# Neighbourhood attention and the filter's small layers run beside two of the three hyena projections, the spectra beside the third; modulation groups are spread over the second block

## The chip, the cores and the metric

One core of a Trainium2 chip runs the whole program in one launch. The metric is device time in microseconds (us) of that core. A core has five engines with queues of their own: TensorE (matmuls; PE, its weight loads PEld), VectorE (DVE), ScalarE (ACT), GpSimd (POOL) and SyncE (SP, which issues nearly all weight loads). Each queue runs in order, and engines wait for one another through semaphores.

## The reference, cut to what matters

Two transformer blocks of two layers each, 256 tokens of width 1024, all float32. Only the even layer (layer 0) of the second block is changed in its computing order; it treats 256 latent and 256 context tokens, 512 columns together:

```python
def na_hyena_mixer(h_lat, h_ctx, ...):                 # layer 0 of the second block
    p = h @ w_in                                       # 1024 x 3072: q, k, v (512 each), x0, x1, v of hyena (512 each)
    a = neighbourhood_attention(qk_norm(q), qk_norm(k), v, k_ctx, v_ctx, rpb)   # 8 heads of 64; context: dense attention
    b = hyena_operator(p[..., 1536:], ...)
    return concatenate([a, b], axis=-1) @ w_out

def hyena_operator(u, conv_w, conv_b, filter_params, d_bias):
    x0, x1, v = split(short_conv(u, conv_w, conv_b), 3)    # taps t-1, t, t+1
    z = v * x1
    filt = hyena_filter(length, *filter_params)            # sin(freq * (h @ fw + fb)) three times, @ fw4, times a window
    y = long_conv(z, filt) + z * d_bias                    # by a Fourier transform: spectra, product, inverse
    return y * x0

# before each layer of the second block, for latent and context alike:
mod = silu(c) @ w_mod[i] + b_mod[i]                    # 1024 x 9216: shift, scale, gate for three places
```

## The kernel before, in words

**Numbers.** Weights and activations of the projections are float32 split into a high and a low float32r part. ACT writes the high part of a weight half block (L1361), DVE the low part (L1651), and TensorE does three matmuls for each 128 x 128 weight tile (L978 to L980): high by high, high by low, low by high. Matmuls of attention, of the filter and of the transforms are plain float32.

**One walk, five engines.** `Engine` holds the order of the work; every engine's class walks it and issues its own instructions, so the order of each queue is the order in which the methods are called. `mark` and `after` turn events into semaphore waits. `fence(who, of)` makes the engines in `who` wait for all that those in `of` have been given so far.

**Projections.** `project_t` (L362) goes through blocks of weights, by default 512 columns by 4 row tiles. Every block has 4 x 4 x 3 = 48 matmuls, and the generator yields after each group of 12. For each finished output tile `evacuate` is called. At the start of a block it calls `paced()` and `prepare`, which loads and splits later blocks. With `wide=256` a block is 256 columns by 8 row tiles: again four yields of 12 matmuls, and an output tile is done at every second yield. Output tiles take PSUM banks from `group` in turn (`Counts.take`); `fresh` waits until the last user of the bank has freed it. There are eight banks of 128 x 512.

**Modulation.** The products with `w_mod` form a generator of 73 steps (`modulations`, L333): 72 times 8 small matmuls on four tiles of `w_mod` (`mod_four`, L1163; 1 MB by four DMAs that SP issues when the last step's matmuls have read the buffers, L2253), every twelfth followed by the closing of a group. `fill(n)` runs n steps; `paced()` runs one at every ninth block (`PACE`); attention pipelines of some stages take them as filler. `modulation(i, j)` (L753) runs steps without pause until group 3i+j is complete, then computes gains, for which ACT waits. Steps 1 to 33 run in the first block of the model.

**The even layer (`even`, L653).** All in one order:
1. q, k, v by `project_t` and `project_n`, banks 0 to 3.
2. The three hyena projections x0, x1, v (two blocks of 48 matmuls each, as q, k and v have; banks 0 to 3). Each output tile goes through `conv`: one ACT instruction with scale and bias (L1540), then two on DVE (L1648) that add the neighbours from the same bank.
3. A fence of all engines, then attention in 16 units (4 pairs of heads by 4 tiles of 128 queries; 512 keys for latent queries, 256 for context ones) through `pipeline` (L307). A unit has six stages, one a round: scores, exp, scale, turn, values, low. In a round the older units go first and a new unit's scores come last. On TensorE a round is: values of unit r-4, turn of unit r-3, scores of unit r. On ACT: copy of values r-4 (L1462), copies of turn r-3 (L1457), the two exponentials of unit r-1 (L1446). On DVE: low part of unit r-5 (L1651, frees the values' bank), reciprocal and diagonals of r-2, bias and maximum of r-1 (L1811, L1813). With `TWO` the scores have two pairs of banks, (3, 4) and (1, 2), the turned halves 5 and 0, the values 6. Every second round has a modulation step (10 in 21 rounds). The scores' weights p have 3 buffers, the turned ones 2. z = v * x1 runs on POOL (L2163) meanwhile.
4. Fences; the loads of the transform matrices, window and filter weights on the ACT queue; z turned (L916); three filter layers, each a matmul (L1214), eight DVE instructions on 64 x 256 (L1941 to L1952) and a sine on ACT (L1549), each followed by a modulation step; the filter's taps (L1224, L1963 to L1967); fence; the spectra of the filter (L1229); fence.
5. `convolution`: spectra of z for both halves s = 0, 1 (L1229), products on DVE (L1989 to L1994) and POOL (L2174, L2176), then the inverse transforms (L1254), each tile followed by three DVE and one ACT instruction (L1648, L2005, L1569, L1651).
6. `modulation(i, 2)` and the output projection "even out", 4 blocks; its rows 0 to 3 are attention's output, 4 to 7 hyena's.

Later, in the odd layer, `modulation(1, 2)` (L753) stands after retention and before the projection "ret out".

**An arrangement like the new one** is in the first block of the model: branch a's attention (`mixing`, L544) with `where=ONE`, scores on one pair of banks (3, 4), runs beside the projections of branch b, 20 groups of 12 matmuls over 13 rounds (256 columns each, half the length of those in the even layer).

Of the kernel before, what the change touches and what calls it, by code (L numbers as in the profile page):

```python
# [109 lines left out]
STRIP, PACE = 266, 9  # L110
# [11 lines left out]
NORM1, NORM2 = 23688, 23552  # L122

# [103 lines left out]
class Engine:  # L227
# [4 lines left out]
    def __init__(self, K, io, mem, banks, sems, e):  # L232
# [8 lines left out]
        self.mod_step, self.fences, self.paces = 0, 0, 0  # L241
# [107 lines left out]
    def paced(self):  # L349

        self.paces += 1
        if self.paces % PACE == 0:
            self.fill(1)
# [299 lines left out]
    def even(self, i, h, N):  # L653
# [7 lines left out]
        OHI, OLO = 4096, 6144  # L661
# [3 lines left out]
        for k, off in enumerate((X0, X1, VV)):  # L665
            run(self.project_t(("hy", k), w, 1536 + 512 * k, 512, h, lambda m, f, k=k, off=off: self.conv(f, A[:, off + m * 512:off + (m + 1) * 512], 4 * k + m)))
        self.fence()
        self.hyena_z()
        rings = self.pair_rings("na", (0, 3072, 24576), 3, 2, 512)
        units = []  # L670
        for r in range(4):
            bi = A[:, 20480 + r * 1024:21504 + r * 1024].rearrange("p (h k) -> p h k", h=2)
            for t in range(4):
                k0, nk = (0, 512) if t < 2 else (256, 256)
                s_ = r * 512 + t * P
                units.append(self.attention(
                    ("na", r, t), A[:, QA + s_:QA + s_ + P], A[:, KA + r * 512 + k0:KA + r * 512 + 512], nk,
                    [A[:, VA + m * 512 + r * P:VA + m * 512 + (r + 1) * P] for m in range(0 if t < 2 else 2, 4)], OHI + s_, OLO + s_, rings,
                    add=bi[:, :, t * 256:(t + 1) * 256] if t < 2 else None, ready="window" if t < 2 else None))
# [12 lines left out]
        cat = self.pair("cat", OHI, OLO, 4, 512)  # L692
        cat2 = self.pair("cat2", 22528, 24576, 4, 512)
        self.convolution(cat2, self.ring("ct", 26624, 2, NT))
        both = self.pair("both", 0, 0, 8, 512)
        both.hi = lambda c, a=0, b=None: (cat.hi(c) if c < 4 else cat2.hi(c - 4))
        both.lo = lambda c, a=0, b=None: (cat.lo(c) if c < 4 else cat2.lo(c - 4))
# [31 lines left out]
    def second_block(self):  # L729
        self.await_context()  # L730
        N = self.norm("second", NORM2, 512)
        for i in range(2):
# [12 lines left out]
            N = self.norm(("b", 0), 8192, 512) if i == 0 else self.norm(("b", 1), NORM2, NT)  # L745
# [147 lines left out]
    load_lambda = load_context = load_window = load_hyena = load_axial = load_decay = await_context = nothing  # L893
    mod_start = mod_four = mod_finish = gains = normed = conv = q_gain = hyena_z = turn_z = filter_layer = filter_end = nothing
    filter_spectra = convolution = axial = silu_out = log_gamma = decay = nothing
# [3 lines left out]
class TensorE(Engine):  # L899
# [296 lines left out]
    def turn_z(self):  # L1196
        for s in range(4):
            f = ("z turn", s)
            out = self.fresh(f, ALL)
            for m in range(4):  # L1200
                mm = self.turn(out[:, m * P:(m + 1) * P], self.A[:, 16384 + m * 512 + s * P:16384 + m * 512 + (s + 1) * P])
            mm.then_inc(*self.mark(("full", f)))

    def filter_layer(self, n):
        e, A, f, FW, HB = self.e, self.A, ("filter", n), 8192, 9664
# [4 lines left out]
        else:  # L1210
            e.wait_ge(*self.after(("filter sin", n - 1)))
            wgt, prev = A[0:64, FW + 256 + 64 * n:FW + 320 + 64 * n], A[0:64, HB + 512 + 256 * ((n - 1) % 2):HB + 768 + 256 * ((n - 1) % 2)]
        out = self.fresh(f, PROJ)[0:64, 0:256]
        e.matmul(out, wgt, prev, start=True, stop=True).then_inc(*self.mark(("full", f)))  # L1214

    def filter_end(self):
        e, A, FW, HB = self.e, self.A, 8192, 9664
        e.wait_ge(*self.after(("filter sin", 2)))
        for m in range(2):
            lt = A[0:64, HB + 512 + m * P:HB + 512 + (m + 1) * P]  # L1220
            for k, way in enumerate(("forward", "backward")):
                f = ("taps", way, m)
                out = self.fresh(f, PROJ)
                e.matmul(out[:, :], lt, A[0:64, FW + 448 + 512 * k:FW + 960 + 512 * k], start=True, stop=True).then_inc(*self.mark(("full", f)))  # L1224

    def forward(self, f, src, kind, n):
        out = self.fresh(f, ALL)
        for m in range(2):
            mm = self.e.matmul(out[:, :], self.A[:, kind * 512 + m * 256 + n * P:kind * 512 + m * 256 + (n + 1) * P], src(m), start=m == 0, stop=m == 1)  # L1229
        mm.then_inc(*self.mark(("full", f)))  # L1230

    def filter_spectra(self):
        A, FIL = self.A, 2048
        self.e.wait_ge(*self.after("dft"))
        for n in range(2):
            for kind in range(2):
                self.forward(("filter spectrum", kind, n), lambda m: A[:, FIL + kind * 1024 + m * 512:FIL + kind * 1024 + (m + 1) * 512], kind, n)

    def convolution(self, cat2, ctb):
        A, ZT = self.A, 18432  # L1240
        for s in range(2):
            for n in range(2):
                for kind in range(2):
# [1137 lines left out]
```

## Time and profile before

| | |
|---|---|
| runs | 3460.04, 3468.54, 3476.8 us; median 3468.54 |
| profiled execution | 3463.9 us, of which the span from first to last instruction is 3462.1 |
| mean granted TensorE clock | 0.949 |
| busy, share of the span | PE 91%, PEld 76%, DVE 48%, ACT 36%, POOL 5% |
| even layer after its norm | from 1752 to 2096 us of the span |
| its hyena projections | about 1821 to 1889 |
| attention | 1889 to 1966 |
| filter to the last inverse transform | 1966 to 2051 |

How to read it: a busy PE is one with matmuls in flight. `PEclk` is the clock that TensorE was granted, 1.00 for 2.4 GHz, 0.50 for 1.2 GHz. In timeline rows the first number is the start in us, the second the length; what stands in brackets is the idle time of the engine before it, and what ended it.

### The profile page before, as it was taken

Reading aid. Unit: us, or ns where it says so; the run is one execution under the profiler, and the core shown is the slowest. Engines: PE = TensorE matmul, PEld = TensorE weight load, DVE = VectorE, ACT = ScalarE, POOL = GpSimd, SP = SyncE. Lnnn points to the kernel's source line nnn. Section 1 sums busy time; section 2 is a strip of 40 time slices with the busy share of each in tenths; the row PEclk is TensorE's granted clock in tenths of the full one; section 3 lists DMA queues with packets and bytes.
Section 4 is the critical chain, followed back from the end, with each engine's and each line's share of the span. In section 5 each row is a group of like instructions: output and inputs, shape, how many; then the busy total and the mean of one; then the engine's idle time right before and its main releaser. Section 6 shows DMA issues by size and latency. Waiting matters only on the chain.

```text
span 3462.1 us, 45581 instructions
## 1 busy us (share of the span) xinstructions
PE 3159.0 (91%) x18558; PEld 2645.2 (76%) x18558; DVE 1673.0 (48%) x2678; ACT 1237.3 (36%) x2073; POOL 161.8 (5%) x181
## 2 busy tenths in 40 slices
PE   6787989987898998999989789999999998996899
PEld 6675979976687997877767457877777777883799
DVE  5554656464565655333374455323443335343465
ACT  4344454433444544222243413212332223233343
POOL 1020000001100000000010010000000000001000
PEclk9898989988999999999999999999999998997999
DMA  4433645642354653232332413233233233241464
GB/s 157 142 104 122 198 166 184 207 159 84 115 187 147 210 197 132 92 110 79 122 125 91 152 47 106 90 109 97 86 122 110 94 108 121 92 158 39 145 204 142
DMA packets 248949, 446.01 MB, mean 129 GB/s; under 512 B 16467, under 2 KB 56804, under 8 KB 247972
## 3 DMA queue, kind: packets, MB, share of 16 engines
q1 hardware_dynamic: 244656, 430.80, 38.4%
q10 hardware_dynamic: 4084, 12.29, 1.0%
q8 instruction: 147, 2.41, 0.3%
q14 instruction: 62, 0.51, 0.0%
HBM read 441.98 MB, written 1.05 MB: 128 GB/s over the span
## 4 chain that ended last, share of the span: by engine, by line
PE 81%; DVE 9%; ACT 4%; issue 2%; DMA 2%; POOL 1%; ACTq 0%; DVEq 0%; POOLq 0%
PE ps L978 22%; PE ps L980 21%; PE ps L979 21%; PE ps L1171 3%; PE ps L1009 2%; PE ps L1010 2%; PE ps L1011 2%; DVE split L1651 2%; DVE AR L1651 1%; PE ps L1119 1%; ACT A L1446 1%; DVE A L1648 1%; DVE A L1701 1%; ACT split L1361 1%; PE ps L1286 1%
## 5 line engine op out<-in xcount | busy, mean ns | idle before, releaser
L978 PE MATMUL ps<-AR,split 128*128 128x256 f32 (+1 forms) x4784 | 1582.0, 331 | 55.2 <-DVE split L1651 36.2
L979 PE MATMUL ps<-AR,split 128*128 128x256 f32 (+1 forms) x4784 | 1560.9, 326 | 0.0
L980 PE MATMUL ps<-AR,split 128*128 128x256 f32 (+1 forms) x4784 | 1559.8, 326 | 0.0
L1651 DVE TENSOR_TENSOR split<-raw,split 128x1024 fp32r<-128x1024 f32 (+2 forms) x712 | 808.0, 1176 | 919.2 <-ACT split L1361 916.9
L978 PEld LDWEIGHTS ps<-AR,split 128*128 128x128 f32 x4784 | 918.2, 192 | 184.1 <-DVE split L1651 41.0
L1361 ACT ACTIVATE split<-raw 128x1024 fp32r<-128x1024 f32 (+2 forms) x712 | 679.9, 1004 | 978.6 <-PE ps L980 846.1
L979 PEld LDWEIGHTS ps<-AR,split 128*128 128x128 f32 x4784 | 919.3, 192 | 83.7 <-issue 1.4
L980 PEld LDWEIGHTS ps<-AR,split 128*128 128x128 f32 x4784 | 919.1, 192 | 82.8
L1648 DVE SCALAR_TENSOR_TENSOR A<-A,ps 128x256 f32<-128x256 f32 (+1 forms) x196 | 96.5, 507 | 129.3 <-ACT A L1404 122.2
L1651 DVE TENSOR_TENSOR AR<-A,AR 128x256 fp32r<-128x256 f32 (+2 forms) x268 | 144.8, 542 | 25.3 <-ACT AR L1420 7.7
L2126 POOL TENSOR_TENSOR A<-A 128x256 f32<-128x256 f32 (+1 forms) x45 | 40.6, 903 | 2091.3 <-ACT A L1369 1987.1
L1408 ACT ACTIVATE AR<-A 128x256 fp32r<-128x256 f32 (+1 forms) x132 | 68.1, 525 | 185.7 <-DVE A L1735 185.6
L1171 PE MATMUL ps<-mod,strip 128*32 128x512 f32 x576 | 106.3, 679 | 20.2 <-DMA mod<-w_mod 13.5
L1404 ACT ACTIVATE A<-ps 128x256 f32<-128x256 f32 (+1 forms) x132 | 63.6, 490 | 146.4 <-PE ps L980 145.9
L1735 DVE TENSOR_TENSOR A<-ps,A 128x256 f32<-128x256 f32 (+1 forms) x132 | 72.0, 555 | 85.7 <-PE ps L980 85.5
L1009 PE MATMUL ps<-split,AR 128*128 128x512 f32 (+1 forms) x288 | 112.4, 390 | 0.0
L1010 PE MATMUL ps<-split,AR 128*128 128x512 f32 (+1 forms) x288 | 109.1, 379 | 0.0
L1011 PE MATMUL ps<-split,AR 128*128 128x512 f32 (+1 forms) x288 | 109.0, 378 | 0.0
L1369 ACT ACTIVATE A<-X 128x256 f32<-128x256 f32 (+1 forms) x112 | 51.7, 476 | 148.5 <-DVE X L1648 134.9
L1648 DVE SCALAR_TENSOR_TENSOR X<-ps,mods,X 128x256 f32<-128x256 f32 x128 | 55.2, 478 | 84.1 <-PE ps L980 84.1
L958 PE MATMUL ps<-AR,split 128*128 128x256 f32 (+1 forms) x176 | 67.6, 394 | 17.5 <-DVE A L1701 11.1
L1105 PE MATMUL ps<-A 64*128 64x256 f32 (+2 forms) x192 | 38.8, 488 | 45.7 <-ACT A L1446 39.8
(229 smaller groups left out, 2235.6 us busy)
## 6 DMA issues: line engine op xcount, KB each, us to landing
mod<-w_mod SPq DMA_DIRECT2D x288, 256.0 KB, 3.9
raw<-w_in SPq DMA_DIRECT2D x120, 512.0 KB, 4.6
raw<-w_gu SPq DMA_DIRECT2D x80, 512.0 KB, 4.7
raw<-ffn_a_in SPq DMA_DIRECT2D x80, 512.0 KB, 4.5
raw<-ffn_b_in SPq DMA_DIRECT2D x80, 512.0 KB, 4.5
raw<-ret_in SPq DMA_DIRECT2D x48, 512.0 KB, 4.6
raw<-w_down SPq DMA_DIRECT2D x44, 512.0 KB, 5.6
raw<-ffn_a_out SPq DMA_DIRECT2D x44, 512.0 KB, 4.4
```

What stands on the lines that cost most here:

```text
L978: e.matmul(out, wh[:, c, m_], x.hi(k0 + c, a, b), start=first, stop=False)
L979: e.matmul(out, wh[:, c, m_], x.lo(k0 + c, a, b), start=False, stop=False)
L980: mm = e.matmul(out, wl[:, c, m_], x.hi(k0 + c, a, b), start=False, stop=last)
L1009: e.matmul(out, x.hi(k0 + c, *s_), wh[:, c, :], start=first, stop=False)
L1010: e.matmul(out, x.hi(k0 + c, *s_), wl[:, c, :], start=False, stop=False)
L1011: mm = e.matmul(out, x.lo(k0 + c, *s_), wh[:, c, :], start=False, stop=last)
L1171: mm = e.matmul(self.bank(f)[32 * t:32 * t + 32, :], self.mem["strip"][:, at:at + 32], self.mem["mod"][t][:, :], start=n == c == 0, stop=n ...
L1361: e.activation(hi, self.raw_view(q), ACT.Copy).then_inc(*self.mark(("w hi", q)))
L1408: self.e.activation(hid.hi(c), th, ACT.Copy).then_inc(*self.mark(("gated hi", bufs.name, k)))
L1648: return self.e.scalar_tensor_tensor(out=out, in0=in0, scalar=scalar, in1=in1, op0=op0, op1=op1)
L1651: return self.e.tensor_tensor(out, v, hi.bitcast(F32), ALU.subtract)
L1735: self.e.tensor_tensor(th, self.bank(f)[:, 0:T], th, ALU.mult).then_inc(*self.mark(("free", f), ("gated", bufs.name, k)))
```

## The change: what it does, and the diff

- `even`: after v's projection comes the fence. The hyena projections of v and x1 (`hyena(2)`, `hyena(1)`) have blocks of 256 columns and banks 0 and 1 only, and are given to `pipeline` as filler, 16 groups of 12 matmuls at 16/20 a round. Attention uses `TRIO`: scores on banks 3 and 4 alone, the turned halves on 5 and 2, values on 6. p has 2 buffers, the turned weights 1. Attention takes no modulation steps.
- `filter_chain` is the pipeline's `side`: loads at round 12, the three filter layers in rounds 15, 18 and 21 (counted from 1), on bank 2, without modulation steps.
- The filter's taps follow; POOL alone waits at a fence and multiplies z; `load_dft`; then `hyena(0)` (x0) runs with `hyena_spectra` between its groups: turns of z, spectra of the filter, spectra of z's first half, on banks 4 to 6.
- Then: products of half 0, spectra of half 1, one modulation step, products of half 1, inverse of half 0, the first block of "even out" (4 groups), inverse of half 1, the rest of "even out", whose tiles take banks 0 to 5.
- Buffers: attention's output goes over q and over the bias; spectra, products, filter, window and transform matrices have new places. The norm ("b", 0) moves from 8192 to 10240.
- `PACE` is 9 in the first block of the model and 4 in the second.

```diff
-STRIP, PACE = 266, 9
+STRIP, PACE = 266, (9, 4)
+TRIO = (((3,), (4,)), (5, 2), (6,))
+HYENA = (4, 5, 6)
     def paced(self):
         self.paces += 1
-        if self.paces % PACE == 0:
+        if self.paces % PACE[self.second] == 0:
             self.fill(1)
     def even(self, i, h, N):
...
-        for k, off in enumerate((X0, X1, VV)):
-            run(self.project_t(("hy", k), w, 1536 + 512 * k, 512, h, lambda m, f, k=k, off=off: self.conv(f, A[:, off + m * 512:off + (m + 1) * 512], 4 * k + m)))
         self.fence()
-        self.hyena_z()
-        rings = self.pair_rings("na", (0, 3072, 24576), 3, 2, 512)
+        def hyena(k, off):
+            return self.project_t(("hy", k), w, 1536 + 512 * k, 512, h, lambda m, f: self.conv(f, A[:, off + m * 512:off + (m + 1) * 512], 4 * k + m), group=(0, 1), wide=256)
+        rings = self.pair_rings("na", (24576, 26624, 14336), 2, 1, 512)
...
-                    add=bi[:, :, t * 256:(t + 1) * 256] if t < 2 else None, ready="window" if t < 2 else None))
-        self.pipeline(units, self.filler, 0.5)
-        self.fence()
-        self.fence(("act",))
-        self.load_hyena()
-        self.turn_z()
-        for n in range(3):
-            self.filter_layer(n)
-            self.fill(1)
+                    add=bi[:, :, t * 256:(t + 1) * 256] if t < 2 else None, ready="window" if t < 2 else None, where=TRIO))
+        beside, side = chain(hyena(2, VV), hyena(1, X1)), self.filter_chain()
+        self.pipeline(units, beside, 16 / 20, side=side)
+        run(beside, side)
         self.filter_end()
-        self.fence()
-        self.filter_spectra()
-        self.fence()
-        self.convolution(cat2, self.ring("ct", 26624, 2, NT))
+        self.fence(("pool",), ("dve",))
+        self.hyena_z()
+        self.load_dft()
+        late = self.hyena_spectra()
+        for _ in hyena(0, X0):
+            next(late, None)
+        run(late)
+        self.fence(("pool",), ("dve",))
...
         self.modulation(i, 2)
-        run(self.project_t("even out", self.io["even_out_2"][0], 0, 1024, both, self.add_mod(i, 5, 512, N), group=WIDE, hurry=True))
+        out = self.project_t("even out", self.io["even_out_2"][0], 0, 1024, both, self.add_mod(i, 5, 512, N), group=(0, 1, 2, 3, 4, 5), hurry=True)
+        self.products(0)
+        for n in range(2):
+            self.spectra(1, n)
+        self.fill(1)
+        self.products(1)
+        self.inverse(0, cat2, ctb)
+        for _ in range(4):
+            next(out)
+        self.inverse(1, cat2, ctb)
+        run(out)
+    def filter_chain(self):
+        for _ in range(11):
+            yield
+        self.load_filter()
+        for n in range(3):
+            for _ in range(3):
+                yield
+            self.filter_layer(n)
+    def hyena_spectra(self):
+        yield
+        for s in range(2):
+            self.turn_z(2 * s)
+            self.turn_z(2 * s + 1)
+            yield
+        for n in range(2):
+            self.filter_spectra(n)
+            yield
+        for n in range(2):
+            self.spectra(0, n)
+            yield
...
+    def products(self, s):
+        e, A = self.e, self.A
+        for n in range(2):
...
+            e.tensor_tensor(y0, z0, h0, ALU.mult).then_inc(*self.mark())
+            e.tensor_tensor(y1, z1, h0, ALU.mult).then_inc(*self.mark())
+            e.wait_ge(*self.own())
+            e.wait_ge(*self.after(("cross", s, n)))
+            e.tensor_tensor(y0, y0, p1, ALU.subtract).then_inc(*self.mark())
+            e.tensor_tensor(y1, y1, p2, ALU.add).then_inc(*self.mark(("product", s, n)))
```

The last method is VectorE's; POOL's part of the products has the same two multiplications for each n as before. `inverse`, `spectra`, `filter_spectra`, `filter_layer` and `filter_end` hold the same instructions as before, by halves or with other addresses; `load_filter` and `load_dft` are `load_hyena` in two parts, each with ACT waiting for its own last instruction first.

## Rows read from the trace of the kernel before

**Rows 1.** The page's busy time of each engine over the whole span.

```profile
PE 3159.0 (91%) x18558; PEld 2645.2 (76%) x18558; DVE 1673.0 (48%) x2678; ACT 1237.3 (36%) x2073; POOL 161.8 (5%) x181
```

**Rows 2.** Busy us by stretch: PE, PEld, DVE, ACT, POOL; then clock, DMA share, GB/s.

```profile
1887.00:1966.00 79.00, 67.77 (x545) 44.03 (x543) 36.89 (x94) 39.86 (x108) 4.51 (x1) 0.96 0.37 121
...
1966.00:2001.00 35.00, 18.45 (x56) 5.67 (x55) 15.51 (x34) 3.62 (x6) 0.00 (x0) 0.74 0.56 186
...
2011.00:2051.00 40.00, 31.18 (x101) 20.23 (x102) 29.91 (x44) 6.32 (x13) 13.30 (x8) 0.96 0.00 0
...
2051.00:2096.00 45.00, 45.00 (x188) 36.09 (x186) 15.78 (x26) 11.83 (x15) 3.87 (x3) 0.96 0.19 59
```

**Rows 3.** Timeline, around a modulation step between two blocks of a projection.

```profile
1876.22 0.40 PE L980 MATMUL ps<-AR,split 128*128 128x512 f32 x1
...
1877.54 0.51 PE L978 MATMUL ps<-AR,split 128*128 128x512 f32 x1
```

**Rows 4.** Timeline, from 3190 us: steps of `modulation(1, 2)`, retention's low parts, "ret out".

```profile
3190.04 1.93 PE L1171 MATMUL ps<-mod,strip 128*32 128x512 f32 x8 [0.78 <-DVE A L2095]
...
3191.26 4.63 DVE L1651 TENSOR_TENSOR AR<-A,AR 128x1024 fp32r<-128x1024 f32 x4 [1.27 <-ACT AR L1630]
...
3221.15 0.36 PE L978 MATMUL ps<-AR,split 128*128 128x256 f32 x1
```

**Rows 5.** Groups of instructions, 1887 to 1966 us, attention: TensorE and ACT.

```profile
L1119 PE MATMUL ps<-A 128*128 128x128 f32 x192 | 27.4, 296 | 0.0
...
L1130 PE MATMUL ps<-A 128*64 128x128 f32 x192 | 14.0, 281 | 5.3 <-DVE AR L1651 3.7 <-ACT A L1457 1.6
...
L1105 PE MATMUL ps<-A 64*128 64x512 f32 x32 | 8.8, 634 | 2.6 <-DVE A L1648 2.6
...
L1457 ACT ACTIVATE A<-ps 128x512 f32<-128x512 f32 x24 | 14.3, 597 | 13.4 <-PE ps L1119 13.4
...
L1446 ACT ACTIVATE A<-ps,small 128x512 f32<-128x512 f32 x16 | 10.8, 682 | 6.4 <-DVE small L1813 6.4
...
L1446 ACT ACTIVATE A<-ps,small 128x256 f32<-128x256 f32 x16 | 7.4, 471 | 0.0
```

**Rows 6.** TensorE's waits in branch a's pipeline, 120 to 185 us: total, times, longest.

```profile
PE ps L1105 <- ACT A L1446: 15.3, 6, 3.8
...
PE ps L1130 <- DVE AR L1651: 4.4, 3, 2.9
```

**Rows 7.** Timeline of the same pipeline, TensorE; and its window.

```profile
153.35 0.78 PE L1105 MATMUL ps<-A 64*128 64x128 f32 x4 [3.17 <-ACT A L1446]
...
166.52 0.44 PE L1130 MATMUL ps<-A 128*64 128x128 f32 x4 [2.93 <-DVE AR L1651]
...
170.53 0.80 PE L1105 MATMUL ps<-A 64*128 64x128 f32 x4 [1.69 <-ACT A L1446]
...
120.00:185.00 65.00, 44.27 (x282) 37.39 (x284) 36.39 (x82) 20.38 (x54) 8.78 (x11) 0.84 0.27 86
```

**Rows 8.** Timeline, last hyena projection to first scores; ACT, TensorE.

```profile
1889.04 0.78 ACT L1540 ACTIVATE A<-ps,cols 128x512 f32<-128x512 f32 x1 [2.02 <-PE ps L980]
...
1891.64 1.56 PE L1105 MATMUL ps<-A 64*128 64x512 f32 x6 [2.64 <-DVE A L1648]
```

**Rows 9.** Timeline: the filter's taps and spectra, TensorE.

```profile
1986.62 0.42 ACT L1549 ACTIVATE A<-A 64x256 f32<-64x256 f32 x1 [4.41 <-DVE A L1952]
...
1994.00 3.70 PE L1224 MATMUL ps<-A 64*128 64x512 f32 x8
...
2000.87 10.09 PE L1229 MATMUL ps<-A 128*128 128x512 f32 x16 [3.17 <-DVE A L1967]
```

**Rows 10.** Groups of instructions, 2011 to 2051 us, spectra, products and inverse.

```profile
L1254 PE MATMUL ps<-A 128*128 128x256 f32 x64 | 16.0, 413 | 4.2 <-DVE A L1994 4.2
...
L1229 PE MATMUL ps<-A 128*128 128x512 f32 x32 | 14.0, 595 | 0.7 <-issue 0.7
...
L1990 DVE TENSOR_TENSOR A<-A 128x512 f32<-128x512 f32 x4 | 7.0, 1754 | 0.0
```

More of the change, by code:

```diff
@@ L729, in second_block @@
     def second_block(self):
+        self.second = 1
         self.await_context()
@@ L1194, in normed, with turn_z @@
         self.late.append(rest)
[L1196 to L1202, printed above, removed]
+    def turn_z(self, s):
+        f = ("z turn", s)
+        out = self.fresh(f, HYENA)
+        self.e.wait_ge(*self.after("z"))
+        for m in range(4):
+            mm = self.turn(out[:, m * P:(m + 1) * P], self.A[:, 16384 + m * 512 + s * P:16384 + m * 512 + (s + 1) * P])
+        mm.then_inc(*self.mark(("full", f)))
     def filter_layer(self, n):
-        e, A, f, FW, HB = self.e, self.A, ("filter", n), 8192, 9664
+        e, A, f = self.e, self.A, ("filter", n)
         if n == 0:
@@ L1230, in forward, with filter_spectra @@
         mm.then_inc(*self.mark(("full", f)))
[L1232 to L1233 removed]
+    def filter_spectra(self, n):
         self.e.wait_ge(*self.after("dft"))
[L1235 to L1255 removed]
@@ new lines, in filter_spectra, with spectra, inverse @@
+        for kind in range(2):
+            self.forward(("filter spectrum", kind, n), lambda m: self.A[:, FIL + kind * 1024 + m * 512:FIL + kind * 1024 + (m + 1) * 512], kind, n, lambda m: ("filter taps", m))
+    def spectra(self, s, n):
+        ZT = 18432
+        for kind in range(2):
+            self.forward(("spectrum", kind, s, n), lambda m: self.A[:, ZT + (2 * s + m) * 512:ZT + (2 * s + m + 1) * 512], kind, n, lambda m: ("free", ("z turn", 2 * s + m)))
+    def inverse(self, s, cat2, ctb):
+        A = self.A
+        for n in range(2):
+            self.e.wait_ge(*self.after(("product", s, n)))
+        for m in range(4):
+            f = ("conv", s, m)
+            out = self.fresh(f, HYENA)[:, 0:NT]
+            for k in range(2):
+                for n in range(2):
+                    o = YS[s][k * 2 + n] + m * P
+                    mm = self.e.matmul(out, A[:, o:o + P], A[:, DFT + (2 + k) * 512 + n * 256:DFT + (2 + k) * 512 + (n + 1) * 256], start=k + n == 0, stop=k + n == 2)
+            mm.then_inc(*self.mark(("full", f)))
@@ L1551, in filter_spectra @@
[L1551 to L1569 removed]
+        self.e.activation(self.A[0:64, SIN + 256 * (n % 2):SIN + 256 + 256 * (n % 2)], self.A[0:64, ARG:ARG + 256], ACT.Sin).then_inc(*self.mark(("filter sin", n)))
@@ new lines, in filter_spectra, with spectra, inverse @@
+    def filter_spectra(self, n):
+        self.keep(("filter spectrum", 1, n), self.A[:, HS + (2 + n) * 512:HS + (3 + n) * 512], 1)
+    def spectra(self, s, n):
+        self.keep(("spectrum", 1, s, n), self.A[:, ZS[s] + (2 + n) * 512:ZS[s] + (3 + n) * 512], 1)
+    def inverse(self, s, cat2, ctb):
+        for m in range(4):
+            k, o = ctb.get()
+            self.e.wait_ge(*self.after(("conv out", s, m)))
+            self.e.activation(cat2.hi(m, s * NT, (s + 1) * NT), self.A[:, o:o + NT], ACT.Copy).then_inc(*self.mark(("conv hi", s, m)))
@@ new lines, in inverse @@
+    def inverse(self, s, cat2, ctb):
+        e, A, X0, X1 = self.e, self.A, 14336, 16384
+        for m in range(4):
+            f, o = ("conv", s, m), m * 512 + s * NT
+            k, ov = ctb.get()
+            cv = A[:, ov:ov + NT]
+            e.wait_ge(*self.after(("full", f)))
+            if ctb.earlier(k):
+                e.wait_ge(*self.after(ctb.earlier(k)))
+            self.stt(cv, A[:, X1 + o:X1 + o + NT], self.cl("hy_bias", m), self.bank(f)[:, 0:NT], ALU.mult, ALU.add).then_inc(*self.mark(("free", f)))
+            e.wait_ge(*self.own())
+            e.tensor_tensor(cv, cv, A[:, X0 + o:X0 + o + NT], ALU.mult).then_inc(*self.mark(("conv out", s, m)))
+            e.wait_ge(*self.after(("conv hi", s, m)))
+            self.low(cat2.lo(m, s * NT, (s + 1) * NT), cv, cat2.hi(m, s * NT, (s + 1) * NT)).then_inc(*self.mark(("cat2", m, s), ctb.freed(k)))
```

187 lines of the change are left out of this document (68 added, 119 removed).

## The prediction

> **What bounds the kernel now.** I read the page first, for the engine that is nearly always busy: TensorE, 91% of the span [rows 1]. So a gain is either TensorE time that disappears or a stretch in which TensorE waits. Then the busy times by stage [rows 2]. Attention: 67.8 of 79 us busy, about 11 us to fill. Filter: 18.5 of 35, with the clock at 0.74, and most of what is busy is modulation steps at half speed. Spectra, products and inverse: 31 of 40, with DVE busy 29.9, so DVE sets the end. The output projection is full: 45.0 us for its 4 blocks, 11.2 a block, 2.8 for a group of 12 matmuls. Last, the place where modulation steps run without pause, each waiting for its DMA [rows 4].
>
> The change fills these holes, so the question is what its own order of waits costs.
>
> **Modulation steps.** There are 73, 33 of them before the second block of the model. By the old pace 17 of the rest are left for the attention stage, the filter and the end: 10, 2 of the filter's 3, and 5 at `modulation(1, 2)`. At every fourth block, the blocks being numbered from the start, the last step falls on block 308, and "g r" ends at 316: nothing is left for `modulation(1, 2)`. Its stretch goes from 3190.0 to 3221.2. Without the steps "ret out" needs the first of retention's four low parts, at 3191.3 + 1.2 = 3192.5 [rows 4]: 28.7 us less. TensorE has been half idle there and would start at the lower clock, so I take 26. Against it stand 17 more steps between the blocks of other projections. One costs 1877.54 - 1876.22 less the usual 0.23 = 1.1 us [rows 3], since its tiles have long landed; at a pace of 4 blocks they have 22 to 45 us for that. 17 x 1.1 = 18.4. SP waits for each step before it issues the next four tiles and then the weights; that happens today and the row shows no wait behind it. Sum: **-7.6 us**. Bounds: -10 (no clock loss) and +5 (0.8 us more for a step, if the extra megabyte delays weights).
>
> **Attention with two projections beside it.** Taken away: 112.1 us from the last matmul of the projections (1888.8) to the filter's first spectrum (2000.9) [rows 8, 9], and 2 x 22.5 us of projections: 157.
>
> TensorE's own work for a unit is (27.4 + 14.0 + 15.5) / 16 = 3.5 us; the 15.5 are 8.8 and 6.7 of scores, the latter for 256 keys [rows 5]. Double-buffered, its scores wait for the exponentials of two units before, and TensorE is nearly full. `TRIO` has one pair of banks: the scores of unit r wait for the exponentials of unit r-1, and on ACT these stand behind the copy of the turned weights r-3, which TensorE has only just finished. From the end of the turn: a copy of 0.60, two exponentials of 0.68 (0.47 with 256 keys) and about 0.2 between them [rows 5]: 2.2 or 1.8 us in every round, and no work beside can cover it, because that work comes after the scores in TensorE's queue. Branch a's pipeline has this arrangement and shows this wait: 15.3 us in 6 rounds, 1.69 at 170.5, 3.17 at 153.4 where DVE was late too [rows 6, 7]. A round is then 3.5 + 2.0 = 5.4 us, and 8.2 with a group of 12 matmuls.
>
> Every second group finishes an output tile. `conv` goes to DVE behind an ACT instruction, and the low part of unit r-5, which frees the only bank of the values, stands behind both DVE instructions. The same evacuation shows 2.64 us from the last matmul to the next possible one [rows 8]; in branch a the same wait is 2.93 [rows 7]. So a round after a finished tile takes 2.6 us more.
>
> - rounds 5 to 16: 12 x 5.4 + 9 groups x 2.8 + 5 x 2.6 = 103
> - rounds 1 to 4, where the first exponentials are waited for in full: 22
> - rounds 17 to 21, 4 groups, and the third filter layer, which nothing covers (4.4 us from a sine to the next, sine 0.4 [rows 9]): 30
> - ACT stands behind DVE's eight instructions of a layer in rounds 15 and 18, and the exponentials' table comes back: 3
> - one modulation step 1.1, the fence 1.5, the taps 3.7 [rows 9]: 6
>
> Together 164. In branch a TensorE had the clock 0.84 over its 65 us [rows 7], in attention before 0.96 [rows 2]; for the new pipeline I take 7 us of loss. **171 against 157: +14.** Bounds of the clock term: 0 and 26 (below).
>
> **x0's projection with the spectra.** 22.5 + 2 (turns of z) + 14.0 (32 matmuls of spectra at full clock [rows 10]) + 1.1 (a step) + 3.5 (waits for z on POOL, changes between kinds) = 43.
>
> **The end of the layer.** From there, on DVE and POOL: products of half 0 until 11; then DVE's copies of spectra, which were queued behind these products, so that the fourth spectrum finds no free bank among three; products of half 1 (1.75 us for a multiplication while POOL runs too [rows 10]) until 21. DVE evacuates the inverse of half 0 only then. TensorE's fourth tile of it waits for that and ends at 25; the first block of "even out" runs to 36.5; the inverse of half 1 (16.0 / 2 = 8.0 [rows 10]) to 44, DVE following; three blocks and a step to 79. So 43 + 79 = 122. Before: 2000.9 to 2096.3 and the projection with its step, 95.4 + 23.6 = 119. **+3**: the block of "even out" that covers DVE pays for what the plain float32 matmuls, now one after another with the projection, cost. Bounds: -8 (POOL's part done early) and +8.
>
> **Moved and free:** the loads of the filter go to ACT's queue in round 12, six issues, some 3 us, hidden as ACT is not half busy [rows 2]; if that cover is gone, one round is 3 us longer. POOL's z now stands in front of the turns; the part of it that is waited for is in the 3.5 above. New addresses and the moved norm: nothing.
>
> **Sum.** -7.6 + 14 + 3 = +9.4, so 3463.9 + 9.4 = 3473.3 for an execution like the profiled one; the median of the runs is 4.6 above it: **3478 us**. The measurement can tell about 0.5% from no change, 17 us: 3451 to 3486.
>
> **Rivals.**
> B, *the work beside covers the waits*. If exponentials and copies ran during the 2.8 us groups, the pipeline would be TensorE's sum: 16 x 3.5 + 45 + start and end 15 + taps, layers and step 8 + changes of kind 6 = 130 instead of 171. For it: ACT and DVE are half idle in attention [rows 2]. Against: the order of the queues, and branch a, where groups beside did not remove the wait [rows 6, 7]. 3478 - 41 = 3437, faster. 20%.
> C, *the clock*, ending slower: gaps of 2 us in every round and of 2.6 in every third hold TensorE's clock where branch a's pipeline has it. At 0.84 a share of 0.32 of 165 us is spent at 1.2 GHz, and half of that, 26 us, is lost where I took 7: 3497. It decides for "slower" once the stretch's clock is below 0.91, a loss of 15. For it: after the gap of 3.17 us branch a's scores took 0.78 [rows 7]. Against: attention before also had short gaps and kept 0.96 [rows 2]. 22%.
> The Trainium skill has a rule that speaks for C (TensorE: Matmul & The Clock Gate, "A second HAM failure mode: psum-queue depth-cycling"): a kernel that cycles through PSUM banks makes TensorE idle briefly between its groups so often that the clock swings between its two levels, and throughput is lost to that. By that rule C's 3497 would be the forecast; the trace agrees for branch a and disagrees for the double-buffered attention.
> D, *the steps do not come free*: spread twice as densely, they cost 2.5 us each, not 1.1, because tiles or weights land late. 17 x 1.4 = 24 more: 3502, slower. Nothing in the rows shows such a wait. 5%. That steps are left over for `modulation(1, 2)` is excluded by the count of blocks.
>
> **How the numbers follow.** Forecast 53% (3463 to 3494 by its bounds), B 20%, C 22%, D 5%. The range takes in B (3437, with its own spread down to 3432) and C and D with theirs: 3432 to 3508; about 2 in 10 lie outside. Faster by over 0.5%: nearly all of B and a little of the forecast, 22%. Slower: most of C, D, and a fifth of the forecast's own spread, 33%. Same: 45%.
>
> **What would show it.** Right: scores (the L1105 of before) wait for ACT's exponentials in nearly every round, 2 us each, some 30 us in all; values wait for DVE's low part about 2.6 us after each finished tile; the stretch from the fence to the taps' end is about 171 us; "ret out" starts about 3 us after retention's last gate; modulation steps never run twice in a row and cost 1.1 us. Wrong: few waits at the scores and a stretch near 130 us (B); a clock below 0.91 there (C); waits for `w_mod` or weights around the steps (D).

## The result and the profile after the change

The changed kernel takes **3494.5 us** (median of 6 runs, 3484.5 to 3506.3); the kernel before took 3471.7 beside it (6 runs, 3455.1 to 3476.9). The ratio is **1.0077**, 95% interval 1.0046 to 1.0109: slower by a little under one per cent. The profiled execution has a span of 3482.7 us against 3462.1, 20.6 more.

The page of the changed kernel first: engines, then two groups (busy, mean ns of one; idle before and what ended it).

```profile
PE 3153.2 (91%) x18558; PEld 2642.4 (76%) x18558; DVE 1678.8 (48%) x2678; ACT 1240.7 (36%) x2075; POOL 158.5 (5%) x181
...
L1146 PE MATMUL ps<-A 64*128 64x256 f32 (+2 forms) x192 | 38.9, 485 | 75.3 <-ACT A L1490 71.0
...
L1212 PE MATMUL ps<-mod,strip 128*32 128x512 f32 x576 | 88.4, 642 | 5.9 <-DMA mod<-w_mod 3.5
```

The engines' sums answer to [rows 1] and hardly differ: TensorE is busy 6 us less and idle 26 us more. Scores are the matmuls on L1146 now, the turn L1160, the values L1171, a modulation step L1212. To see where the idle time is, take busy us by stretch, as in [rows 2]: the attention with its two projections and the filter; x0's projection with spectra; the end of the layer.

```profile
1819.00:2011.80 192.80, 130.30 (x664) 91.95 (x663) 66.55 (x141) 60.11 (x130) 0.00 (x0) 0.84 0.12 38
2011.80:2053.20 41.40, 40.44 (x153) 26.71 (x153) 19.38 (x19) 7.83 (x11) 5.42 (x1) 0.97 0.20 64
2053.20:2135.00 81.80, 72.94 (x305) 52.69 (x304) 46.60 (x72) 18.17 (x28) 15.51 (x11) 0.94 0.20 65
```

The first stretch is the answer: 192.8 us, 62.5 of them idle, and a clock of 0.84. The other two are full or nearly so. What TensorE waited for in 1819 to 2001 us (total, times, longest):

```profile
PE ps L1146 <- ACT A L1490: 34.1, 15, 5.2
PE ps L1171 <- DVE AR L1685: 21.9, 8, 3.3
```

And TensorE's timeline at some of these places, at the taps (L1265), at the fourth spectrum of half 1 (L1271) and at the start of "ret out":

```profile
1826.25 2.08 PE L1146 MATMUL ps<-A 64*128 64x512 f32 x4 [5.18 <-ACT A L1490]
...
1851.93 1.13 PE L1146 MATMUL ps<-A 64*128 64x512 f32 x4 [1.69 <-ACT A L1490]
...
1858.69 1.09 PE L1171 MATMUL ps<-A 128*64 128x128 f32 x16 [2.64 <-DVE AR L1685]
...
2004.65 7.19 PE L1265 MATMUL ps<-A 64*128 64x512 f32 x8 [5.59 <-ACT A L1591]
...
2067.40 3.78 PE L1271 MATMUL ps<-A 128*128 128x512 f32 x4 [8.83 <-DVE A L1746]
...
3240.25 0.55 PE L1019 MATMUL ps<-AR,split 128*128 128x256 f32 x1 [3.47 <-DVE AR L1685]
```

The scores of all 15 units after the first wait for the exponentials of the unit just before, and the values wait for the low part that stands behind `conv` on DVE. Both are what [rows 6, 7] showed of branch a. The taps, which took 3.70 us in [rows 9], take 7.19 after an idle 5.59: the granted clock there is 0.50, the lower level. "ret out" now starts after a wait of 3.47 us for retention's low part, with no modulation step ahead of it. Outside the layer: the projection of the values ends at 1818.9 us, where it ended at 1820.4 in the execution before, and from the end of the even layer to the end the changed kernel needs 15.8 us less. The even layer in between takes 37.9 us more.

### The profile page after: what moved, and what is told of

Same layout as the page of the kernel before. It is cut to its first block, busy times and chain, and to the rows that moved or that the text cites. A ratio compares the mean times of both kernels' runs of the same rounds, so it can differ in the third digit from the quotient of the medians.

```text
span 3482.7 us, 45577 instructions
## 1 busy us (share of the span) xinstructions
PE 3153.2 (91%) x18558; PEld 2642.4 (76%) x18558; DVE 1678.8 (48%) x2678; ACT 1240.7 (36%) x2075; POOL 158.5 (5%) x181
## 3 DMA queue, kind: packets, MB, share of 16 engines
q1 hardware_dynamic: 247728, 430.80, 37.9%
## 4 chain that ended last, share of the span: by engine, by line
PE 81%; DVE 10%; ACT 4%; issue 2%; DMA 2%; POOL 1%; ACTq 0%; DVEq 0%; POOLq 0%
PE ps L1019 22%; PE ps L1020 21%; PE ps L1021 21%; PE ps L1212 2%; DVE split L1685 2%; PE ps L1050 2%; PE ps L1052 2%; PE ps L1051 2%; PE ps L1160 1%; DVE AR L1685 1%; ACT A L1490 1%; DVE A L1682 1%; ACT split L1405 1%; PE ps L1146 1%; DVE A L1735 1%
## 5 line engine op out<-in xcount | busy, mean ns | idle before, releaser
L1146 PE MATMUL ps<-A 64*128 64x256 f32 (+2 forms) x192 | 38.9, 485 | 75.3 <-ACT A L1490 71.0
L1212 PE MATMUL ps<-mod,strip 128*32 128x512 f32 x576 | 88.4, 642 | 5.9 <-DMA mod<-w_mod 3.5
```

The lines of the kernel that those rows point to most:

```text
L1146: mm = self.e.matmul(outs[h], q[64 * h:64 * h + 64, :], k[64 * h:64 * h + 64, :], start=True, stop=True)
L1212: mm = e.matmul(self.bank(f)[32 * t:32 * t + 32, :], self.mem["strip"][:, at:at + 32], self.mem["mod"][t][:, :], start=n == c == 0, stop=n ...
```

## The experiments

Stretches are compared, not spans. Executions drift apart by more than the effects asked for: in two runs below, ScalarE's order and both orders, the first scores come 18 to 19 us later than in the changed kernel, after the same instructions. A run that stands for itself therefore tells little, and its windows tell more. "The stretch" is from the fence ahead of the first scores to the first matmul of x0's projection. Idle is the length of a window less TensorE's busy time in it.

**The pace alone.** The kernel before, with

```diff
-STRIP, PACE = 266, 9
+STRIP, PACE = 266, (9, 4)
-        if self.paces % PACE == 0:
+        if self.paces % PACE[self.second] == 0:
```

> The kernel before with the new pace alone: a modulation step at every fourth block from the second block of the model on, everything else as it was. Theory (the prediction's first term): the 17 steps of modulation(1, 2) are done before it is reached, 'ret out' starts about 28.7 us sooner after retention, each step that is moved costs 1.1 us where it now stands, so the whole is 8 us shorter than the kernel before, bounds 10 shorter and 5 longer. Rival: what the change of the whole program shows, a rest of the program (from the end of the even layer to the end) that is 15.8 us shorter, comes from the pace, and the steps that stand before the even layer are no dearer: then about 14 us shorter. Second rival: steps spread twice as densely delay weights: 2.5 us each, 16 us longer.

Measured: 3451.1 us against 3459.6, ratio 0.997 (0.9944 to 0.9996), so some 10 us less, and its profiled span is 8.2 shorter than that of before. "ret out" starts at

```profile
3209.39 0.55 PE L979 MATMUL ps<-AR,split 128*128 128x256 f32 x1 [3.48 <-DVE AR L1652]
```

against 3221.15 in [rows 4]: 11.8 sooner in the program: what is left of the 28.7 saved there after what the moved steps cost ahead of it. The first term of the sum holds, and the second rival is excluded. The first rival's 14 us lies inside the interval, but its premise does not hold in the trace: from 1420 to 1821 us, ahead of the even layer, the steps are ten instead of five and TensorE is busy with them for 10.7 us instead of 5.3.

**The old pace in the changed kernel.** `PACE = 266, (9, 9)` in place of (9, 4).

> The changed kernel with the old pace, a step at every ninth block throughout. The change took away the twelve steps that the attention and the filter of the kernel before had beside them, so 17 steps that the new pace spreads would be met all at once where the modulation is needed. Theory: each costs there what the five bare ones cost before retention's output, (3221.15 - 3192.5) / 5 = 5.7 us with its wait for the load, instead of 1.1: 17 x 4.6 = 78 us more than the changed kernel, about 3572 us. Rival: the loads of the bare steps run ahead over the whole of what stands before, so that only the first few wait: 17 x 1.5 = 25 us more, about 3520.

Measured: 3587.6 us, one run, 93 more; the theory said 78, its rival 25. The group of the steps and its waits, and one step:

```profile
L1212 PE MATMUL ps<-mod,strip 128*32 128x512 f32 x576 | 131.4, 718 | 47.7 <-DMA mod<-w_mod 44.5
```

```profile
PE ps L1212 <- DMA mod<-w_mod: 44.5, 17, 3.2
...
2902.67 3.92 PE L1212 MATMUL ps<-mod,strip 128*32 128x512 f32 x8 [2.88 <-DMA mod<-w_mod]
```

Seventeen steps are met bare, as counted, in three places: four from 2479 us, seven from 2892 and six from 3306. The first of each place finds its tiles; the other 14 wait about 2.9 us and then take 3.1 to 4.6 us instead of 1.1, since their weight loads wait again for one tile after the other. (That the view counts 17 waits as well is chance: two are those that the changed kernel has too, and one step waits twice.) Together that is 41 us more of waiting than in the changed kernel and 43 more of busy time. The new pace is therefore no addition that could be left out: the change took the steps' old places away.

**One pair of score banks, nothing else.** The kernel before with its attention on `TRIO`:

```diff
-... ready="window" if t < 2 else None))
+... ready="window" if t < 2 else None, where=TRIO))
```

> The kernel before with one pair of score banks instead of two in the neighbourhood attention, no projection beside it (modulation steps as before, rings as before). Theory: scores wait for the exponentials of the unit just before in nearly every round, 2 us each, 15 of them; attention takes 79 + about 25 = 104 us, and because of these gaps the clock falls from 0.96 to about 0.86 in it, which takes 5 us more. Rival: the new waits take the place of the 11 us that are idle there today: 79 + 18 = 97 us or less, and the clock stays above 0.92, so that the low clock of the changed kernel comes from the projections beside and not from the single pair.

Measured: 3494.1 us, one run, against 3459.6 of the kernel before beside it. From the last projection matmul to the filter's first 120.1 us, where before has 88.5; first the window and the wait of this kernel, then the window of before.

```profile
1888.70:2008.80 120.10, 74.50 (x554) 47.10 (x554) 38.64 (x94) 42.03 (x110) 4.50 (x1) 0.88 0.31 104
```

```profile
PE ps L1106 <- ACT A L1447: 31.5, 15, 5.2
```

```profile
1889.00:1977.50 88.50, 68.00 (x554) 44.52 (x553) 36.77 (x94) 42.21 (x110) 4.51 (x1) 0.93 0.42 141
```

So the single pair costs 31.6 us by itself: 25.1 in idle time, 6.5 in busy time of the same 554 matmuls. The theory's numbers are met (25 and 5 were expected), and the idle time of before did not take the new waits in. The clock falls with no projection beside it, from 0.93 to 0.88 in these windows. And the exponentials have three buffers here, as before, so the scores' waits do not come from the two of the changed kernel.

**ScalarE's order.** The changed kernel with the newest unit's exponentials ahead of the older copies, on ACT alone, and a third buffer for them. To make room the filter's last weights go to another place and are loaded later, and the load of the transform matrices waits for the taps:

```diff
+            if early and self.name == "act":
+                for u in new:
+                    next(u)
+                last, live = new, live[:len(live) - len(new)]
...
-rings = self.pair_rings("na", (24576, 26624, 14336), 2, 1, 512)
+rings = self.pair_rings("na", (24576, 26624, 14336), 3, 1, 512)
+rings[0].get = spread(rings[0], (24576, 25600, 15360))
```

> The changed kernel, in which ScalarE takes the exponentials of the newest unit before the copies of the older ones, with a third buffer for the exponentials (the filter's last weights are loaded later, to another place, to make room). Theory: the wait of the scores (34.1 us, 15 times) falls below 6 us, since the exponentials now run beside the values and the turn; the values' waits for DVE's low part (21.9 us, 8 times) stay; with more than half of the gaps gone the clock of the stretch rises from 0.86 to about 0.92; from the fence to the end of the taps 193 - 29 - 10 = about 154 us. Rival: the gaps of the values alone hold the clock at 0.86: 193 - 29 = 164 us. Second rival: the copies, now later, make the values wait instead, and the stretch stays at 185 or more.

**DVE's order.** The changed kernel with DVE's part of `conv` held back until the units of the next round have been advanced:

```diff
-        self.stt(d3[:, :, 1:NT], ...)
+        self.held.append(rest)
...
+            for f in self.held or []:
+                f()
             if side is not None:
                 next(side, None)
```

> The changed kernel, in which DVE's two instructions of a finished projection tile stand behind the next round's low part, sum and maximum instead of ahead of them. Theory: the values' waits (21.9 us, 8 times) fall below 4 us, the scores' wait stays at about 34 us, and the stretch from the fence to the end of the taps is 193 - 18 - 3 = about 172 us at a clock of about 0.88. Rival: the exponentials come later by nothing and the scores, now reached earlier, wait longer by what the values no longer wait: the stretch stays at 185 or more.

**Both orders.**

> The changed kernel with both orders mended: ScalarE's exponentials ahead of its copies (with the third buffer) and DVE's part of a projection tile behind the next round's low part. Alone the first took the stretch from the first scores to the first matmul of x0's projection from 192 to 171 us, the second to 168, both at a clock of 0.82 to 0.85. Theory A (gaps add up, the clock stays where it is as long as the round is made of short matmuls): 168 - 19 = about 149 us, clock 0.80 to 0.86. Theory B (the clock comes back once nearly all gaps are gone): 0.93 or more and about 135 us. Either way the run is near the kernel before: 3494 - 43 = 3451 by A, 3437 by B.

The windows of the stretch: ScalarE's order, then DVE's, then both.

```profile
1836.80:2008.90 172.10, 130.73 (x663) 92.45 (x662) 66.38 (x141) 57.65 (x128) 0.00 (x0) 0.82 0.11 36
```

```profile
1821.40:1990.40 169.00, 125.29 (x662) 86.84 (x662) 67.70 (x141) 59.54 (x130) 0.00 (x0) 0.85 0.13 43
```

```profile
1837.80:1975.30 137.50, 115.00 (x663) 79.98 (x663) 66.63 (x141) 56.45 (x128) 0.00 (x0) 0.91 0.15 45
```

And TensorE's waits for ACT's exponentials and for DVE's low part, in the same order:

```profile
PE ps L1188 <- DVE AR L1707: 22.4, 8, 3.8
PE ps L1163 <- ACT A L1512: 12.2, 7, 5.2
```

```profile
PE ps L1155 <- ACT A L1499: 31.4, 15, 5.2
PE ps L1180 <- DVE AR L1694: 6.1, 3, 3.3
```

```profile
PE ps L1172 <- ACT A L1521: 9.2, 7, 5.2
PE ps L1197 <- DVE AR L1716: 6.4, 4, 4.1
```

Each order takes away most of its own wait and leaves the other: 34.1 us at the scores becomes 12.2 with ScalarE's order, 21.9 at the values becomes 6.1 with DVE's. The two mechanisms are separate and both are shown.

ScalarE's order gave 20.7 us of the stretch. 172.1 is neither the theory's 154 nor its rival's 164: the scores kept 12.2 us of wait, not under 6, and the clock did not rise. Its one run, 3489.6 us, lies within the runs of the changed kernel, so the gain shows in the window alone. DVE's order gave 23.8 us; 169.0 meets the theory's 172, with 6.1 us of wait left instead of under 4 and a clock of 0.85 instead of 0.88. Its one run is 3462.8.

Together they gave 55.3, and 3437.1 us in all, ratio 0.9925 to before (0.9902 to 0.9948). By its time this is theory B (135 and 3437) and not A (149 and 3451); its clock, 0.91, lies between A's 0.86 and B's 0.93. Idle time adds up: 62.5 us in the changed kernel, 41.4 and 43.7 with one order, 22.5 with both, which is 21 and 19 less, and 40. Busy time does not: 130.3, then 130.7 and 125.3, then 115.0, for the same work. These 15 us are the clock, and two thirds of them came only when most of both kinds of gap were gone. How far one profile can be trusted in this: the run with the old pace has the same pipeline as the changed kernel and shows 192.7 us at 0.82 for it, against 192.8 at 0.84. So 0.82 to 0.85 cannot be told apart; 0.91, with 0.93 in both profiles below that have both orders, can.

**The filter's layers closer together, a group in round 1.** On top of both orders: `for _ in range(2)` in place of 3 in `filter_chain`, and `owed` starting at 0.2. The filter's last weights are loaded one layer later than with both orders.

> The kernel with both orders mended, and two smaller things: the filter's layers two rounds apart instead of three (rounds 14, 16, 18), and the first group of a projection already in round 1. Theory: the third sine is ready before the taps are reached, so the 5.4 us of idle ahead of them go, and with it the low clock at which the taps' eight matmuls take 7.2 us instead of 3.6; the group in round 1 hides 2.8 of the 5.2 us for which the second scores wait. From the first scores to the first matmul of x0's projection 137 - 5 - 3.6 - 2.8 = about 125 us; the run 3437 - 11 = about 3426 us. Rival: DVE's eight instructions of a layer, now closer together, come in front of the maxima and low parts of three units that are in full flow, and make scores and values wait by what the end saves: 134 us or more.

```profile
1825.40:1957.60 132.20, 111.45 (x662) 78.84 (x662) 66.00 (x141) 58.52 (x130) 0.00 (x0) 0.93 0.15 47
```

Measured: 132.2 us for the stretch and 3430.6 for the run, ratio 0.9906 (0.9873 to 0.9940), which overlaps that of both orders alone. The wait ahead of the taps falls from 5.4 us to 1.1, but scores wait 11.9 us where they waited 9.2, and one low part is still 4.2 late: 132.2 is nearer to the rival's 134 than to the theory's 125. The last run below has the same pipeline, and its stretch takes 133.0 us at the same clock, 0.93.

**Two projections ahead, two pairs of score banks.** The changed kernel with

```diff
+        run(hyena(2, VV), hyena(1, X1))
         self.fence()
...
-... where=TRIO))
-        beside, side = chain(hyena(2, VV), hyena(1, X1)), self.filter_chain()
-        self.pipeline(units, beside, 16 / 20, side=side)
+... where=TWO))
+        self.pipeline(units, side=side)
```

> The changed kernel, but the projections of v and x1 (hyena(2), hyena(1)) stand ahead of the attention again, at full width, and the attention has its two pairs of score banks back; the filter's layers stay beside it, no modulation step is in it; x0's projection with the spectra, the end of the layer and the pace as in the changed kernel. Theory (the single pair and its gaps are what the change pays): from the end of the values' projection to the end of the taps 45 us for the two projections, about 70 for the attention (79 before, with ten modulation steps in it), about 13 for the third filter layer and the taps: 128 us where the changed kernel takes 193 and the kernel before 157; the clock in the attention is 0.93 or more; the run about 3494 - 65 = 3430 us, faster than both. Rival: without modulation steps between them the short matmuls of the attention have gaps of their own and the clock falls below 0.88: then 140 us and 3442.

Then the same with modulation steps beside it, `self.pipeline(units, self.filler, 0.5, side=side)`:

> The kernel with two projections ahead of a double-buffered attention (attention to the end of the taps took 99.2 us at a clock of 0.79, 71.8 of it busy), with modulation steps put back beside it, one in every second round as in the kernel before. Theory: the attention's short matmuls alone leave gaps that hold the clock down; ten steps of about 1.1 us fill them, the clock returns to 0.90 or more, the stretch takes about 97 us although it holds ten steps more, and these ten steps, 11 us, are missing from the rest of the program: about 3441 - 12 = 3429 us. Rival: the steps do nothing for the clock (below 0.84) and add their time here as they save it there: 110 us for the stretch, and 3441 for the run.

The projections and the attention of the first, its attention again in two parts, up to the filter's first matmul and after it; then the attention of the second:

```profile
1828.20:1874.30 46.10, 46.10 (x201) 35.92 (x199) 19.82 (x22) 13.86 (x16) 0.00 (x0) 1.00 0.35 114
1874.30:1973.50 99.20, 71.79 (x463) 48.97 (x462) 47.11 (x119) 45.89 (x114) 0.00 (x0) 0.79 0.07 20
...
1874.30:1936.30 62.00, 46.98 (x341) 33.47 (x340) 30.32 (x73) 32.11 (x88) 0.00 (x0) 0.88 0.05 14
1936.30:1973.50 37.20, 24.80 (x122) 15.51 (x122) 16.79 (x46) 13.78 (x27) 0.00 (x0) 0.64 0.09 29
```

```profile
1884.60:1985.50 100.90, 78.51 (x551) 48.14 (x550) 47.45 (x121) 46.73 (x115) 0.00 (x0) 0.87 0.41 129
```

The first takes 145 us from the values' projection to the end of the taps, not 128: the rival (140) was nearer, with a clock lower still than it said. Its run is 3441.2 us, ratio 0.9927 (0.9899 to 0.9955), faster than both kernels all the same. With the steps the stretch grows by 1.7 us though 88 matmuls more run in it, busy only 6.7 us longer, and the run is 3432.2 us, ratio 0.9916 (0.9881 to 0.9951); the two intervals overlap, so the 9 us between the runs are not shown. The clock rose to 0.87, between theory and rival. It is not the 0.96 of [rows 2], but most of what is missing lies behind the filter's first matmul. Ahead of it the attention had 0.88 without the steps and 0.92 with them; behind it 0.64 and 0.78. In that second part of the first run the values wait 7.7 us in 3 places for their low part, which stands behind the filter's instructions on DVE, and the taps wait 3.7 us for the last sine. This is read from the traces; no run leaves the filter out.

**The end of the layer.** On top of the filter's closer layers:

```diff
-        self.products(0)
         for n in range(2):
             self.spectra(1, n)
+        self.products(0)
         self.fill(1)
         self.products(1)
-        self.inverse(0, cat2, ctb)
         for _ in range(4):
             next(out)
+        self.inverse(0, cat2, ctb)
         self.inverse(1, cat2, ctb)
```

> The kernel with both orders mended and the filter's layers closer together, and in the end of the layer two moves: DVE copies the spectra of half 1 before it takes the products of half 0, and the first block of the output projection, which needs only the attention's outputs, stands ahead of both inverses instead of between them. Theory (the end of the layer is held by DVE, and the block is the only work that covers it): the 8.8 us for which TensorE waits with the fourth spectrum go, both inverses find their products and free banks, and the end of the layer takes 79.4 - 8.8 = about 71 us; the run 3430 - 9 = about 3422 us. Rival: the wait moves to the inverse of half 0, whose tiles DVE frees only after the products of half 1: then 76 us or more for the end and no gain that can be told.

```profile
2002.00:2075.30 73.30, 71.03 (x306) 52.03 (x304) 46.64 (x72) 18.15 (x28) 15.38 (x11) 1.00 0.23 72
```

The changed kernel's 81.8 us for this (to the sums of the next norm) are 73.3 now: 8.5 less, with the clock at 1.00 instead of 0.94. The wait for the fourth spectrum is gone. That is the theory, whose 71 us end with the last block of the projection: 71.1 to there. The kernel that it builds on also takes 81.8. The run is **3425.3 us**, ratio **0.9875** (0.9848 to 0.9902): 1.25% faster than the kernel before, and the fastest of these kernels. From the kernel that it builds on it is told apart by the window, not by the runs, whose intervals overlap.

## Why the prediction was right, and which term failed

The range held the time, and slower had its third of the chances; the likeliest number, 3478, was 16 us too low, and the mechanism that came true is that of a rival with 22%. The range, 3432 to 3508, was wide enough to take in every rival, so that the time fell into it says little. Part of it is luck besides: ahead of the even layer the changed kernel's execution was 1.5 us shorter, where five more steps should have made it 5.5 longer, and these 7 us hid part of the 19 by which the layer exceeded its forecast (37.9 us more than before, against 14 + 3 and two moved steps). By its own steps:

- **Modulation, -7.6: right.** By itself (the first run above) the pace gave -8.2 between two profiles and some 10 in the runs. In the changed kernel the steps have 17.9 us less of busy time and 14.3 less of waiting than before, and the rest of the program after the even layer is 15.8 shorter, where the forecast's 26 less ten moved steps at 1.1 give 15.
- **Waits of the pipeline: right, in place and size.** Forecast: 2 us at the scores in every round, some 30 in all; measured 34.1, of which 5.2 are the start. Forecast: 2.6 at the values after a finished tile; measured 21.9 in 8, 2.7 each.
- **The clock of the pipeline, 7 us: the step that failed.** The stretch took 192.9 us, not 171, at a clock of 0.84. Between 0.84 and 0.93 the same matmuls lost 18.9 us (130.3 against 111.5 busy). In proportion the 0.16 missing in the changed kernel cost about 33, an estimate from these two windows; the prediction's own price for that clock, under rival C, was 26. The sum without the clock was 164, and with either it comes to 190 or 197: the rest of the sum holds within a few us, and the 7 was the term that did not. I had set branch a's 0.84 [rows 7] against the double-buffered attention's 0.96 [rows 2] and gone by the second, though the new pipeline shares its single pair with the first. The row nearest in mechanism was the one to take.
- **x0's projection with spectra, 43, and the end, 79: right** (41.4, and 79.4 from the end of that stretch to the last block's end at 2132.7, with the 8.8 us wait of the fourth spectrum behind the products).
- **Rival C, 3497: this is what happened**, 2.5 us from its price. Its condition, a clock under 0.91, is met. Its cause is narrowed by the runs: the gaps at scores and values hold the clock down, and either kind alone is enough for that (0.82 and 0.85 in one execution each). The filter's layers run beside the attention in all of these kernels, so they are not what separates 0.84 from 0.91.
- **Rival B, 3437: not this kernel.** With both orders mended the run does take 3437.1, but with a stretch of 137.5 us and not B's 130, so that the two numbers are the same is in part chance. The work beside covers most of the waits once no queue puts older work in front.
- **Rival D: excluded.** The steps wait 3.5 us for their loads in all.
- **A reading that its rows do not show:** that bare steps wait for their loads. The one step shown in [rows 4] waits for DVE. It is so all the same for the four behind it, which wait 2.8 us each for `w_mod`.

The Trainium skill's rule (TensorE: Matmul & The Clock Gate, "A second HAM failure mode: psum-queue depth-cycling") foretold C: short idle gaps between groups that cycle through PSUM banks swing the clock. The trace agrees for this kernel, with 0.84. With both orders mended the banks are cycled just as before and the clock is 0.91, so it is the gaps that count.

What made the change lose: the idle time that it could fill was 11, 17 and 9 us in three stretches [rows 2], and it paid for that with a pair of banks (31.6 us when that alone is taken), with DVE's two `conv` instructions in front of the low parts (21.9 us of waits), and with the clock that both cost.

## What to carry to other kernels

When work is laid beside a pipeline, count the banks that it takes: if double buffering is what pays, every round waits for the stage behind it, and nothing beside covers that unless the queues let the newest stage go first. Order matters per engine: ACT's exponentials ahead of older copies and DVE's bulk work behind the small instruction that frees a bank made 55 us of a stretch of 193 here, with the same work. And price the clock from the row with the same waits, not from the row with the same instructions.

## What was not expected of the hardware

- The clock did not follow the idle time in proportion. With 62.5 us idle of 193 it was 0.84, with 41 of 172 it was 0.82, with 44 of 169 it was 0.85, with 22.5 of 137.5 it was 0.91, and with 20.8 of 132.2 it was 0.93.
- The double-buffered attention kept 0.96 with modulation steps beside it [rows 2], and again in the run with the new pace alone. With the filter in place of the steps the whole stretch had 0.79, with both 0.87, and most of the difference lies behind the filter's first matmul (0.64 and 0.78, against 0.88 and 0.92 ahead of it). The filter's layers are small on TensorE, but where they run the values wait behind DVE's instructions for them. That this is what lowers the clock there is likely from the traces and not shown by a run.
- Same instructions, other executions: the stretch from 800 to 1000 us, in a part of the program that the change leaves alone, had a clock of 0.90 in the profile of before and 0.94 in that of the changed kernel. That may be why the values' projection ends 1.5 us sooner in the changed kernel, in spite of the five steps more that the new pace puts ahead of it.
